# One block for adaLN conditioning and input projection, a third buffer of query weights, and 45 instead of 33 expert groups in the first tile's own routing

## The chip, the core and the metric

The kernel runs on one core of one Trainium2 chip. The metric is device time in microseconds for one execution. Five engines run their own instruction streams and meet at semaphores: TensorE (PE, with its weight loads as PEld), VectorE (DVE), ScalarE (ACT), GpSimd (POOL) and SyncE (SP), which only issues transfers. Sixteen DMA engines serve all transfers. All arithmetic is in 32-bit floats.

## What is computed

One layer of a decoder trunk, for 1024 prompt rows and for 32 sampled rows (8 sequences of 4), d_model = 1024. Cut to what matters here:

```
mod = c @ w_ada + b_ada            # 9 rows of c: one for the prompt, 8 for the sampled rows
shift1, scale1, gate1, shift2, scale2, gate2 = split(mod, 6)       # 1024 columns each
h = rms(x) * norm1_g * (1 + scale1) + shift1
q, k, v, f, glu = split(h @ w_in, [512, 1024, 1536, 1544])         # 2568 columns
A = forgetting attention over 8 heads of 64 (q and k normed, f gives the decay)
B = silu(layernorm(causal depthwise conv, 31 taps (a * sigmoid(b)))),   a, b = split(glu)
x1 = x + gate1 * (concat(A, B) @ w_o)
h2 = rms(x1) * norm2_g * (1 + scale2) + shift2
y = x1 + gate2 * peer(h2)

peer(h): per row and each of 8 retrieval heads:
    q = h @ w_query[head]                         # 256 columns
    the 16 best of 128 x 128 product keys -> 16 experts out of 16384, with softmax gates g
    sum over the 128 (head, expert) pairs of  g * gelu(h . expert_u[e]) * expert_v[e]
```

The experts are gathered from memory row by row: one row is expert_u and expert_v of one expert, 8 KB.

## The kernel before

Four functions run one after the other, each a block of its own with a stream for each engine; a block ends only when all its engines are done.

`condition` computes mod. SyncE loads w_ada in 12 chunks of 2 MB into three buffers `wa` (L112); TensorE makes 9 x 512 products (L157), VectorE copies them to `mod` (L187), TensorE transposes them into columns (`to_columns`, L147). Then VectorE adds the bias (`modT`, L190) and makes (1 + scale) * norm_g (`sgT`, L193 and L194). The two gates are spread over 128 rows for the prompt (L169) and over 32 rows for the sampled rows (L177) by TensorE, copied by VectorE (L202, L207) and stored (L119, L120). w_in, 10.3 MB, is issued as one transfer behind w_ada (L114).

`project` computes the norm, the modulation and h @ w_in, first for the 32 sampled rows, then for eight tiles of 128 prompt rows: `norm_x` on ScalarE and VectorE, `rows_up` (L555, transposes of x), the modulation into `hT` (VectorE at L459 and L462 for the sampled rows, ScalarE at L399 for prompt rows), then on TensorE the f columns (L572), q, k, v (L578), the two halves of the GLU columns (`gated`, L562) with `rows_up` of the next tile between them, and the transposes of q and k (L605, for the sampled rows L609), which ScalarE copies to `qTb` and `kTb` (L408, L412) for SyncE to store.

`sampled` does the attention of the sampled rows over their paged cache.

`tail` does all the rest. `iterate` writes one order for all engines: a tile has 55 steps (attention in 0 to 15, convolution, output product and norm in 16 to 34, routing from S_ROUTE = 35 on). Each tile's steps run beside the expert groups of the tile before: `PLAN` says how many of its 128 groups follow each step. A group is one gather of 128 expert rows (L1108, GpSimd, 1 MB, into one of the 8 slots of `ring`), a dot product on VectorE (L1515), gelu, gate and a diagonal on ScalarE (L1227, L1229, L1237) and four 128 x 64 matmuls on TensorE (L1670). A slot is free for the next gather when its matmuls are done. The first tile has no tile before it; `PLAN_0` puts groups of its own behind its last steps: as soon as head 0 has its experts and gates they begin, 33 in all, and the second tile's steps run beside the 95 that are left. In the routing TensorE needs the query weights of one head, 1 MB, every second step (L1651). `load_wq` on SyncE loads them (L994) into two buffers, each as soon as the head two before has been multiplied (`qd_done`). SyncE's order in a tile is: keys of heads 2 to 7, x, the eight weight loads, then `prefetch` of the next tile (q, mask, conv rows, the first two key loads), then the store of y.

The lines of this order that the change touches:

```python
PLAN_0 = [0] * (S_GATE + 1) + [2] * 12 + [3] * 3          # 33 groups

def load_wq(t, h):                                         # SyncE
    n = H * t + h
    if n >= 2:
        sp.wait_ge(qd_done, n - 1)
    sp.dma_start(wq[n % 2][:, :, :], ...).then_inc(wq_in[n % 2], 16)
```

Of the kernel before, what the change touches and what calls it, by code (L numbers as in the profile page):

```python
# [78 lines left out]
def condition(nc, I, S, K, w_in_load):  # L79
    with ExitStack() as ctx:  # L80
        sb = lambda n, s, d=F32: ctx.enter_context(nc.sbuf_tensor(n, s, d))
        sem = lambda n: ctx.enter_context(nc.semaphore(n))
        wa = [sb(f"wa{i}", [P, DC, 512]) for i in range(3)]
        cT = sb("cT", [P, DC, M])
        bT = sb("bT", [P, 48])
        ng = sb("ng", [P, 2, DC])
        gS, gate, gate_s = sb("gS", [P, 2, DC, TS]), sb("gate", [P, 2, D]), sb("gate_s", [TS, 2, D])
        mod = sb("mod", [M, 6 * D])
        wide = sb("wide", [P, 2 * SEQ - P], BF16)
        mod_bank = ctx.enter_context(nc.psum_tensor("mod_bank", [P, 512], F32))  # L90
        mod_ps = mod_bank[:, 0:48 * M].rearrange("p (n m) -> p n m", m=M)
        row_ps = [ctx.enter_context(nc.psum_tensor(f"row_ps{i}", [P, 512], F32)) for i in range(3)]
        gate_ps = [ctx.enter_context(nc.psum_tensor(f"gate_ps{i}", [P, 512], F32)) for i in range(4)]
        ada_in = [sem(f"c_w{i}") for i in range(3)]
        rows_copied, modT_done = sem("c_rows"), sem("c_modT")
        small_in, w_used, id_step = sem("c_small"), sem("c_used"), sem("c_id")
        own_v, gates, gates_out = sem("c_own"), sem("c_gates"), sem("c_gout")
        stored = sem("c_stored")
        wv = I["w_ada"].rearrange("(k p) n -> p k n", p=P)
        modT, sgT, ident = K["modT"], K["sgT"], K["ident"]  # L100
        NCH = 12
        block = ctx.enter_context(nc.Block())

        @block.sync
        def _(sp):
            sp.dma_start(cT[:, :, :], I["cT"]).then_inc(small_in, 16)
            sp.dma_start(bT[:, :], I["b_adaT"]).then_inc(small_in, 16)
            sp.dma_start(ng[:, :, :], I["norm_gT"]).then_inc(small_in, 16)
            for n in range(NCH):
                if n >= 3:  # L110
                    sp.wait_ge(w_used, n - 2)
                sp.dma_start(wa[n % 3][:, :, :], wv[:, :, n * 512:(n + 1) * 512]).then_inc(ada_in[n % 3], 16)  # L112

            sp.dma_start(K["w_in"][:, :, :], I["w_in"].rearrange("(k p) n -> p k n", p=P)).then_inc(w_in_load, 16)  # L114
            sp.wait_ge(id_step, 7)
            sp.dma_start(S["mask"], wide[:, :]).then_inc(stored, 16)
            sp.wait_ge(gates_out, 2)
            for g in range(2):
                sp.dma_start(S["gate"][g], gate[:, g, :]).then_inc(stored, 16)  # L119
                sp.dma_start(S["gate_s"][g], gate_s[:, g, :]).then_inc(stored, 16)  # L120
            sp.wait_ge(stored, 16 * 5)

        @block.gpsimd
        def _(pool):

            pool.memset(ident[:, :], 0.0).then_inc(id_step, 1)
            pool.memset(K["tri"][:, :], 1.0).then_inc(id_step, 1)
            pool.memset(K["ones"][:, :], 1.0).then_inc(id_step, 1)
            pool.memset(wide[:, :], 0.0).then_inc(id_step, 1)
            pool.wait_ge(id_step, 4)  # L130
            pool.affine_select(out=ident[:, :], in_=ident[:, :], compare_op=ALU.not_equal, fill=1.0, base=0,
# [1651 lines left out]
```

## Time and profile before

| | |
|---|---|
| median of 3 runs | 3870.56 us (3864.44 to 3872.29) |
| the profiled execution | 3873.22 us |
| its span, from first to last instruction | 3871.5 us |
| mean granted TensorE clock | 0.908 of full |
| TensorE busy | 3115.4 us |
| VectorE busy | 2471.7 us |
| ScalarE busy | 1550.2 us |
| GpSimd busy | 1283.3 us |
| DMA | 1291.75 MB, mean 334 GB/s over the span |

Busy time is the time in which an engine has an instruction under way. A window's row has, for each engine, its busy time and in brackets the number of its instructions, then the granted TensorE clock as a share of full speed, the mean busy share of the 16 DMA engines, and what they moved. The DMA share can come out at 1.01 or 1.02; that is full. In the page's rows of 40 slices a slice is 96.8 us, a digit the busy share in tenths (9 is 90% or more).

By the rows of the timeline, `condition` runs to about 122 us, `project` to about 530, `sampled` to 645, and `tail` from there; the first tile's routing ends at about 870, and a tile of the tail then takes some 370 us.

### The profile page before, as it was taken

Reading aid. Unit: us, or ns where it says so; the run is one execution under the profiler, and the core shown is the slowest. Engines: PE = TensorE matmul, PEld = TensorE weight load, DVE = VectorE, ACT = ScalarE, POOL = GpSimd, SP = SyncE. Lnnn points to the kernel's source line nnn. Section 1 sums busy time; section 2 is a strip of 40 time slices with the busy share of each in tenths; the row PEclk is TensorE's granted clock in tenths of the full one; section 3 lists DMA queues with packets and bytes.
Section 4 is the critical chain, followed back from the end, with each engine's and each line's share of the span. In section 5 each row is a group of like instructions: output and inputs, shape, how many; then the busy total and the mean of one; then the engine's idle time right before and its main releaser. Section 6 shows DMA issues by size and latency. Waiting matters only on the chain.

```text
span 3871.5 us, 44083 instructions
## 1 busy us (share of the span) xinstructions
PE 3115.4 (80%) x11624; PEld 1421.8 (37%) x11624; DVE 2471.7 (64%) x6411; ACT 1550.2 (40%) x4275; POOL 1283.3 (33%) x1139
## 2 busy tenths in 40 slices
PE   8699976578887887788688868887887788757877
PEld 2466742333342243224332433343334333411341
DVE  0222323488588677767776777587668766856785
ACT  0234411246425533543355345534552555233423
POOL 0000030034334343444344334443343334344433
PEclk9699987699998998899899989998998899979989
DMA  8211152389999999999999999999999999989998
GB/s 317 86 47 41 41 200 96 132 320 399 367 376 366 414 404 375 371 413 407 371 401 409 408 355 404 408 401 378 400 398 403 341 407 405 380 338 418 417 377 355
DMA packets 299720, 1291.75 MB, mean 334 GB/s; under 512 B 39270, under 2 KB 135414, under 8 KB 163124
## 3 DMA queue, kind: packets, MB, share of 16 engines
q0 software_dynamic: 156672, 1124.27, 72.3%
q1 hardware_dynamic: 142780, 164.51, 12.9%
q8 instruction: 93, 1.52, 0.2%
q14 instruction: 175, 1.43, 0.1%
HBM read 1271.34 MB, written 17.79 MB: 333 GB/s over the span
## 4 chain that ended last, share of the span: by engine, by line
DMA 34%; PE 21%; DVE 14%; issue 7%; ACT 5%; SPq 1%; POOL 1%; DVEq 0%; POOLq 0%; ACTq 0%
DMA ring<-experts_dram,idxc 22%; DMA wq<-w_query_dram 12%; PE YY L1670 12%; DVE ring L1515 5%; PE M L1651 4%; PE TT L1657 3%; DVE yac L1262 2%; SPq L1021 1%; ACT gw L1229 1%; ACT dg L1237 1%; ACT L1227 1%; DVE yac L1436 1%; PE SS L1546 1%; ACT ga L1227 1%; POOL ring L1108 1%
## 5 line engine op out<-in xcount | busy, mean ns | idle before, releaser
L1670 PE MATMUL YY<-ring,dg 128*64 128x512 f32 (+1 forms) x4224 | 1804.1, 655 | 486.0 <-ACT dg L1237 463.3
L1108 POOL DMA_INDIRECT ring<-experts_dram,idxc x1056 | 1233.4, 1168 | 1810.3 <-PE YY L1670 1608.0
L1515 DVE CUSTOM_DVE_ANT_0 ring<-ring,h2c 128x1024 f32<-128x1024 f32 x1056 | 1273.3, 1226 | 551.6 <-DMA ring<-experts_dram,idxc 542.2
L1670 PEld LDWEIGHTS YY<-ring,dg 128*64 128x64 f32 (+1 forms) x4224 | 502.1, 145 | 1576.3 <-ACT dg L1237 831.2
L1227 ACT ACTIVATE ga<-act 128x1 f32<-128x1 f32 x1056 | 210.6, 199 | 911.5 <-DVE act L1515 909.1
L1651 PE MATMUL M<-fT,wq 128*128 128x128 f32 (+1 forms) x2304 | 310.2, 299 | 96.3 <-DMA wq<-w_query_dram 96.3
L1237 ACT ACTIVATE dg<-fold,gw 128x64 f32<-128x64 f32 x1024 | 356.0, 348 | 51.0 <-ACT gw L1229 2.6
L1651 PEld LDWEIGHTS M<-fT,wq 128*128 128x128 f32 x2304 | 297.4, 213 | 155.7 <-DMA wq<-w_query_dram 122.4
L1229 ACT ACTIVATE gw<-ga,gc 128x1 f32<-128x1 f32 x1056 | 311.0, 295 | 35.1 <-ACT ga L1227 1.0
L1262 DVE SCALAR_TENSOR_TENSOR yac<-win,cw,yac 128x128 f32<-128x128 f32 x960 | 262.9, 346 | 2.5 <-issue 2.5
L1188 ACT ACTIVATE qh<-M 128x256 f32<-128x256 f32 x64 | 24.5, 383 | 462.4 <-PE M L1651 462.4
L578 PE MATMUL A<-w_in,hT 128*128 128x512 f32 (+1 forms) x432 | 193.5, 609 | 3.6 <-ACT kTb L408 3.6
L688 POOL DMA_INDIRECT pages<-cache_dram,k_idx x32 | 30.2, 944 | 408.2 <-POOLq L213 398.8
L1657 PE MATMUL TT<-w_o,fT 128*128 128x512 f32 (+1 forms) x288 | 138.5, 627 | 10.1 <-DVE fT L1437 6.8
L562 PEld LDWEIGHTS A<-hT,w_in 128*128 128x128 f32 x1152 | 141.1, 205 | 4.2 <-issue 4.2
L562 PE MATMUL A<-hT,w_in 128*128 128x128 f32 (+1 forms) x1152 | 141.9, 286 | 0.0
L1227 ACT ACT_TABLE_LOAD x96 | 123.2, 1283 | 13.0 <-DVE act L1515 11.4
L578 PEld LDWEIGHTS A<-w_in,hT 128*128 128x128 f32 (+1 forms) x432 | 79.2, 185 | 111.1 <-issue 106.9
L1546 PE MATMUL SS<-kh,t_qT 66*128 66x512 f32 (+1 forms) x192 | 88.0, 570 | 25.8 <-ACT h2c L1214 16.2
L1555 PEld LDWEIGHTS V<-V,t_PT 128*128 128x128 f32 x656 | 79.6, 194 | 52.2 <-issue 45.4
L157 PE MATMUL row_ps<-wa,cT 128*9 128x512 f32 x192 | 86.1, 603 | 10.3 <-DMA wa<-w_ada_dram 10.3
L1555 PE MATMUL V<-V,t_PT 128*128 128x64 f32 x656 | 88.8, 283 | 4.8 <-DMA V<-v_prompt_dram_out 4.4
(305 smaller groups left out, 2385.9 us busy)
## 6 DMA issues: line engine op xcount, KB each, us to landing
wq<-w_query_dram SPq DMA_DIRECT2D x72, 1024.0 KB, 27.0
wa<-w_ada_dram SPq DMA_DIRECT2D x12, 2048.0 KB, 7.9
ring<-experts_dram,idxc POOLq DMA_INDIRECT x1056, 13.7
w_in<-w_in_dram SPq DMA_DIRECT2D x1, 10272.0 KB, 34.1
kh<-kT_scratch SPq DMA_DIRECT2D x16, 264.0 KB
xb<-x_prompt_dram SPq DMA_DIRECT2D x8, 512.0 KB, 5.3
t_xb<-x_prompt_dram SPq DMA_DIRECT2D x8, 512.0 KB, 11.1
w_o<-w_o_dram SPq DMA_DIRECT2D x8, 512.0 KB, 5.5
```

The source lines that it names most:

```text
L562: mm = pe.matmul(A[half][:, (j % CC) * P:(j % CC) * P + r], w_in[:, k, ZG + j * P:ZG + (j + 1) * P], h[:, k, 0:r], start=(k == 0), stop=(k ...
L578: mm = pe.matmul(A[2 + j][0:r, :], h[:, k, 0:r], w_in[:, k, j * DA:(j + 1) * DA], start=(k == 0), stop=(k == DC - 1))
L1108: pool.indirect_dma_start(ring[:, k % RING, :], None, I["experts"], bass.IndirectOffsetOnAxis(idxc[:, k:k + 1], 0)).then_inc(g_in[k % RING ...
L1227: act.activation(ga[:, a:a + 1], act8[:, a:a + 1], ACT.Gelu).then_inc(gelu_done, 1)
L1229: act.activation(gw[:, a:a + 1], ga[:, a:a + 1], ACT.Copy, scale=gc[:, k:k + 1]).then_inc(gelu_done, 1)
L1237: act.activation(dg[:, k % DG, :], fold2[:, :], ACT.Copy, scale=gw[:, a:a + 1]).then_inc(diag_done, 1)
L1262: own.step(v.scalar_tensor_tensor(out_of(c), rows_of(c, k), cw[:, c, k:k + 1], out_of(c), ALU.mult, ALU.add))
L1515: v.tensor_tensor_reduce(out=u, in0=u, in1=h2, scale=1.0, scalar=0.0, op0=ALU.mult, op1=ALU.add, accum_out=act8[:, k % RING:k % RING + 1]) ...
L1555: mm = pe.matmul(V0[:, h * HD:(h + 1) * HD], PTs[:, b * P:(b + 1) * P], V[:, b, h * HD:(h + 1) * HD], start=(b == 0), stop=(b == nk // P - 1))
L1651: mm = pe.matmul(M0[:, g * P:g * P + r], wq[h % 2][:, k, g * NK:(g + 1) * NK], fT[:, k, 0:r], start=(k == 0), stop=(k == DC - 1))
L1657: mm = pe.matmul(TT[0:r, g * 512:(g + 1) * 512], fT[:, k, 0:r], w_o[:, k, g * 512:(g + 1) * 512], start=(k == 0), stop=(k == DC - 1), skip ...
L1670: mm = pe.matmul(YY[o, half * 512:(half + 1) * 512], dg[:, k % DG, 0:w], ring[:, k % RING, D + half * 512:D + (half + 1) * 512], start=(k ...
```

## The change

It has three parts.

1. `condition` and `project` become one block, `front`. `condition` no longer opens a block: it returns pieces of each engine's stream, which `front` places. The norm of x_sample runs at the start; `rows_up(0)`, its transposes, stands between the last row product and `to_columns(11)`. w_in is issued in nine pieces: the q, k, v and f columns of one 128-row slab behind each of the last eight w_ada chunks, and the GLU columns behind them. The gates are no longer spread on TensorE: 16 transposes give 9 rows of each gate, four copies put them where `qTb` and `kTb` will be, and the stores read one row 128 times (the prompt) or each of 8 rows 4 times (the sampled rows). TensorE waits for these copies ahead of the q, k, v product of the sampled rows; ScalarE waits for these stores ahead of its first write to `qTb`. `mod` holds two chunks instead of twelve and lies in `sqq`. VectorE waits for the projection's constants behind the norm of the first prompt tile, and makes the page indices behind the sampled rows.
2. `PLAN_0` has 3 groups behind each of its last 15 steps, 45 in all; the second tile's steps run beside 83.
3. The query weights have three buffers, head h in h % 3. The third shares its memory with the two key buffers `kh`: its load for head 2 waits until all scores of the tile are done, and the keys of the next tile wait for head 5's query.

The diff, cut to its core:

```diff
-def condition(nc, I, S, K, w_in_load):
+def condition(nc, ctx, I, S, K, R):
+    A, mod, gate = R["A"], R["mod"], R["gate"]
+    mod_ps = A[4][:, 0:48 * M].rearrange("p (n m) -> p n m", m=M)
+    row_ps, gate_ps = A[0:3], A[0:4]
...
             sp.dma_start(wa[n % 3][:, :, :], wv[:, :, n * 512:(n + 1) * 512]).then_inc(ada_in[n % 3], 16)
-            sp.dma_start(K["w_in"][:, :, :], I["w_in"].rearrange("(k p) n -> p k n", p=P)).then_inc(w_in_load, 16)
+            if n >= NCH - DC:
+                k = n - NCH + DC
+                sp.dma_start(K["w_in"][:, k, 0:ZG], wi[:, k, 0:ZG]).then_inc(R["w_qkv"], 16)
+        sp.dma_start(K["w_in"][:, :, ZG:DIN], wi[:, :, ZG:DIN]).then_inc(R["w_glu"], 16)
...
+        rows_up(0)
+        to_columns(NCH - 1)
+        pe.wait_ge(own_v, 1)
+        for g, first in ((0, 16), (1, 40)):
+            for half in range(2):
+                for c in range(4):
+                    mm = pe.transpose(gate_ps[2 * g + half][0:M, c * P:(c + 1) * P], modT[:, first + 4 * half + c, :],
+                                      ident[:, :])
+        mm.then_inc(modT_done, 1)
...
+    def vector_gates(v):
+        v.wait_ge(modT_done, NCH + 1)
+        for g in range(2):
+            for half in range(2):
+                v.tensor_copy(gate[g][0:M, half * 512:(half + 1) * 512], gate_ps[2 * g + half][0:M, :])\
+                    .then_inc(rows_copied, 1)
+    def store_gates(sp):
+        sp.wait_ge(rows_copied, NCH + 4)
+        for g in range(2):
+            sp.dma_start(S["gate"][g].unsqueeze(0), gate[g][0:1, :].unsqueeze(1).to_broadcast([1, P, D]))\
+                .then_inc(gates_out, 16)
+            sp.dma_start(S["gate_s"][g].rearrange("(n q) d -> n q d", q=QS),
+                         gate[g][1:M, :].unsqueeze(1).to_broadcast([NS, QS, D])).then_inc(gates_out, 16)
...
+    def gates_stored(eng):
+        eng.wait_ge(gates_out, 16 * 5)
+    def gates_read(eng):
+        eng.wait_ge(rows_copied, NCH + 4)
...
             sp.dma_start(xb[0:TS, :], I["x_sample"]).then_inc(x_in, 16)
+            c_sync(sp)
...
             load_x(1, 0)
+            store_gates(sp)
             store(0, 1, None, None)
...
                 if not isinstance(t, int) or t > 0:
                     act.wait_ge(stored_qk, 32 * t)
+                else:
+                    gates_stored(act)
...
                 if r == TS:
+                    c_rows(v)
...
                     v.sem_inc(hT_ready, 1)
+                    c_gates(v)
                 if more:
                     norm_x(t + 1)
...
                 if some(t):
                     pe.wait_ge(qkT_ready, t)
+                else:
+                    gates_read(pe)
...
+                if not some(t):
+                    pe.wait_ge(w_glu, 16)
                 gated(1, r, h)
...
-            pe.wait_ge(w_in_load, 16)
-            rows_up(0)
+            c_tensor(pe, rows_up)
+            pe.wait_ge(w_qkv, 16 * DC)
...
-PLAN_0 = [0] * (S_GATE + 1) + [2] * 12 + [3] * 3
+PLAN_0 = [0] * (S_GATE + 1) + [3] * 15
...
-        wq = [sb(f"wq{i}", [P, DC, 2 * NK]) for i in range(2)]
+        shared = sb("shared", [P, 2 * SEQ])
+        wq = [sb(f"wq{i}", [P, DC, 2 * NK]) for i in range(2)] + [shared[:, :].rearrange("p (k n) -> p k n", k=DC)]
-        kh = [sb(f"kh{i}", [AUG, SEQ]) for i in range(2)]
+        kh = [shared[0:AUG, i * SEQ:(i + 1) * SEQ] for i in range(2)]
...
             def load_wq(t, h):
-                n = H * t + h
-                if n >= 2:
-                    sp.wait_ge(qd_done, n - 1)
-                sp.dma_start(wq[n % 2][:, :, :], wqv[:, :, h * 2 * NK:(h + 1) * 2 * NK]).then_inc(wq_in[n % 2], 16)
+                b = h % 3
+                if h > 2:
+                    sp.wait_ge(qd_done, H * t + h - 2)
+                elif b == 2:
+                    sp.wait_ge(s_done, H * min(t + 1, NB))
+                elif t:
+                    sp.wait_ge(qd_done, H * t - 1 + b)
+                sp.dma_start(wq[b][:, :, :], wqv[:, :, h * 2 * NK:(h + 1) * 2 * NK]).then_inc(wq_in[b], 16)
...
                     sp.wait_ge(conv_done, t)
+                    sp.wait_ge(qd_done, H * t - 2)
...
-                    pe.wait_ge(wq_in[h % 2], 64 * t + 16 * (h // 2 + 1))
+                    b = h % 3
+                    pe.wait_ge(wq_in[b], 16 * ((2 if b == 2 else 3) * t + h // 3 + 1))
```

## Rows read from the trace of the kernel before

**Rows 1.** the page: DMA row in 40 slices; one line of its costliest groups
```profile
DMA  8211152389999999999999999999999999989998
...
L157 PE MATMUL row_ps<-wa,cT 128*9 128x512 f32 x192 | 86.1, 603 | 10.3 <-DMA wa<-w_ada_dram 10.3
```

**Rows 2.** windows by stage: busy time of each engine, granted clock, DMA share, GB/s
```profile
760.00:880.00 120.00, 85.81 (x313) 39.68 (x314) 102.40 (x333) 53.51 (x139) 40.91 (x38) 0.87 0.90 333
880.00:1185.00 305.00, 247.10 (x898) 105.24 (x896) 230.42 (x621) 139.84 (x381) 112.10 (x101) 0.93 0.96 372
1185.00:1555.00 370.00, 300.29 (x1028) 125.75 (x1028) 267.85 (x673) 163.76 (x475) 148.97 (x130) 0.91 1.00 398
```

**Rows 3.** timeline of TensorE: start, length, line, what, count [idle before <- releaser]
```profile
99.83 0.41 PE L147 MATMUL mod_bank<-ident,mod 9*128 9x9 f32 x4 [0.43 <-DVE mod L187]
...
136.50 1.03 PE L555 MATMUL A<-ident,xs 32*128 32x32 f32 x8 [22.78 <-DVE xs L445]
...
141.27 23.66 PE L578 MATMUL A<-w_in,hT 128*32 128x512 f32 x48
...
177.82 13.70 PE L562 MATMUL A<-hT,w_in 128*128 128x32 f32 x64
...
240.12 20.87 PE L578 MATMUL A<-w_in,hT 128*128 128x512 f32 x48 [0.45 <-ACT kTb L408]
```

**Rows 4.** timeline of VectorE, and of SyncE's queue in the last row
```profile
100.28 0.61 DVE L190 TENSOR_TENSOR modT<-mod_bank,bT 128x432 f32<-128x432 f32 x1 [0.51 <-PE mod_bank L147]
...
113.76 2.82 DVE L207 COPY gate_s<-gate_ps 32x512 f32<-32x512 f32 x4 [5.50 <-PE gate_ps L177]
...
140.09 0.19 DVE L462 TENSOR_TENSOR hT<-hT,modT 128x32 f32<-128x32 f32 x1
...
77.58 0.58 SPq L114 DMA_DIRECT2D w_in<-w_in_dram  x1
```

**Rows 5.** DMA issues: queue, count, KB each, median us from issue to landing
```profile
wq<-w_query_dram SPq DMA_DIRECT2D x72, 1024.0 KB, 27.0
wa<-w_ada_dram SPq DMA_DIRECT2D x12, 2048.0 KB, 7.9
...
w_in<-w_in_dram SPq DMA_DIRECT2D x1, 10272.0 KB, 34.1
...
gate_scratch<-gate SPq DMA_DIRECT2D x2, 512.0 KB, 3.5
```

**Rows 6.** windows in the front
```profile
40.00:60.00 20.00, 20.00 (x57) 4.71 (x56) 2.04 (x3) 0.00 (x0) 0.00 (x0) 1.00 0.82 279
95.00:100.00 5.00, 4.57 (x17) 1.21 (x15) 0.68 (x1) 0.00 (x0) 0.00 (x0) 1.00 1.01 427
170.00:175.00 5.00, 5.00 (x25) 5.00 (x25) 3.54 (x10) 2.45 (x3) 0.00 (x0) 0.50 0.00 0
```

**Rows 7.** timeline of VectorE: one head in the first tile's routing
```profile
802.73 0.49 DVE L1285 MAX8 best<-sc 128x8 f32<-128x128 f32 x2
...
805.94 1.22 DVE L1515 CUSTOM_DVE_ANT_0 ring<-ring,h2c 128x1024 f32<-128x1024 f32 x1
...
818.49 0.48 DVE L1285 MAX8 best<-sc 128x8 f32<-128x128 f32 x2
```

**Rows 8.** TensorE's waits (us, times, longest); windows at two of the stalls
```profile
PE M L1651 <- DMA wq<-w_query_dram: 96.3, 18, 10.0
...
1480.00:1490.00 10.00, 10.00 (x43) 7.26 (x43) 3.94 (x7) 2.16 (x9) 1.12 (x2) 0.74 0.72 266
3690.00:3700.00 10.00, 10.00 (x30) 4.84 (x32) 1.80 (x12) 3.80 (x15) 1.87 (x2) 0.65 0.79 256
```

**Rows 9.** timeline of GpSimd at a tile's boundary; windows at two boundaries
```profile
1567.16 0.94 POOL L1108 DMA_INDIRECT ring<-experts_dram,idxc  x1 [17.23 <-PE YY L1670]
...
1160.00:1175.00 15.00, 6.19 (x13) 1.95 (x12) 13.52 (x37) 5.57 (x13) 4.36 (x4) 0.77 0.50 186
3770.00:3780.00 10.00, 7.45 (x20) 3.08 (x22) 7.95 (x19) 8.06 (x22) 4.45 (x4) 0.73 0.53 194
```

More of the change, by code:

```diff
@@ L213, in project, with front @@
+def front(nc, I, O, S, K):
     with ExitStack() as ctx:
@@ L255, in project @@
         ident = K["ident"]
+        w_qkv, w_glu = sem("p_wqkv"), sem("p_wglu")
+        flat = lambda a: a[:, :, :].rearrange("p h t -> p (h t)")
+        c_sync, c_gpsimd, c_tensor, c_rows, c_gates, store_gates, gates_stored, modulation_ready, gates_read = condition(
+            nc, ctx, I, S, K, {"A": A, "mod": sqq[:, :].rearrange("p (g n) -> p g n", g=2),
+                               "gate": [flat(qTb), flat(kTb)], "w_qkv": w_qkv, "w_glu": w_glu})
         block = ctx.enter_context(nc.Block())
@@ L314, in _ @@
             sp.dma_start(O["conv_prompt"], ub[P - (W - 1):P, :]).then_inc(once_out, 16)
+            gates_stored(sp)
             sp.wait_ge(once_out, 16 * 3)
@@ L321, in _ @@
         def _(pool):
+            c_gpsimd(pool)
             pool.memset(zero[:, :, :], 0.0).then_inc(cst, 1)
@@ L397, in body @@
                     act.wait_ge(xT_done, t + 2)
+                    if not some(t):
+                        modulation_ready(act)
                     for c in range(DC):
@@ L414, in body @@
                 a.then_inc(qkT_ready, 1)
+            norm_x(0)
             act.wait_ge(own_p, 5)
-            norm_x(0)
             body(0, 0)
@@ L465, in body @@
                     v.sem_inc(hT_ready, 1)
+                    c_gates(v)
                 if more:
                     norm_x(t + 1)
+                if not some(t):
+                    v.wait_ge(own_p, 5)
+                    v.wait_ge(small_in, 80)
                 own.start(OVN * (t + 2) + OV * t if more else OVN * (t + 1) + OV * t)
@@ L527, in body @@
                 assert own.n == OV, own.n
-            v.wait_ge(own_p, 5)
-            v.wait_ge(small_in, 80)
+            norm_x(0)
+            body(0)
             v.wait_ge(paged, 1)
@@ L535, in _ @@
                 .then_inc(lane_ready, 1)
-            norm_x(0)
-            body(0)
             body(1)
@@ L584, in body @@
                     u_rows(TS)
+                if not some(t):
+                    pe.wait_ge(w_glu, 16)
                 gated(1, r, h)
@@ L965, in tail @@
         k_in = [sem(f"k{i}") for i in range(2)]
-        wq_in = [sem(f"wq{i}") for i in range(2)]
+        wq_in = [sem(f"wq{i}") for i in range(3)]
         smp_in, gate_in = sem("smp"), sem("gate")
@@ L1732, in build @@
                     K[name] = early.enter_context(nc.sbuf_tensor(name, shape, F32))
-                condition(nc, I, S, K, w_in_load)
-                project(nc, I, O, S, K, w_in_load)
+                front(nc, I, O, S, K)
             sampled(nc, I, O, S, K)
```

195 lines of the change are left out of this document (75 added, 120 removed).

## The prediction

> **What bounds the kernel now.** I read the page's DMA row first [rows 1], then the time by stage [rows 2], and only then single instructions. The DMA row says that there are two kernels in this one. From slice 9 on it stands at 9 in almost every slice; before that it mostly doesn't. The stage table gives the same in numbers: from 1185 to 1555 us, one whole tile of prompt rows in the tail, the DMA share is 1.00 at 398 GB/s, and so it goes for seven tiles. A tile takes 128 gathers of 128 rows of 8 KB (1.05 MB each) and eight 1 MB weight loads, and its length is what the DMA engines need for these bytes. A faster step in there is worth only the DMA idle time that it removes. From 760 to 880 us, the routing of the first tile, the share is 0.90. Between 110 and 530 us (digits 1 and 2 of the DMA row) the front runs on TensorE, with the DMA engines hardly used.
>
> So I price each part in one of two ways: in the front by the chain of instructions that leads to the projection, in the tail by DMA idle time, with a share of 1.00 as full.
>
> **Part 1, one block.** Now: the columns of the last row product are transposed at 99.83 to 100.24, then TensorE does gates only, and it is idle for 22.8 us before 136.50; the first q, k, v product begins at 141.27 [rows 3]. In between lie the gates, their stores, the end of the block, a new load of x_sample and its norm. The changed chain, step by step. Loading x_sample first puts one issue ahead of the weights: +0.4. Eight transposes of x_sample (1.03 at 136.50) go between the last product and the last columns, where TensorE waits 0.43 for a copy: +0.6 at most, I take 0.3. So modT starts at 100.28 [rows 4] + 0.7 = 101.0 and takes 0.61; four operations on a sixth of its elements have to follow, an estimate of 0.25 each: 102.6. The sixteen operations that modulate the sampled rows run from the end of their transposes at 137.5 to 140.28, 2.7 us: 105.3. The new wait of TensorE for the gate copies stands ahead of q, k, v; behind it on TensorE is everything. VectorE makes these four copies behind the modulation, 2.8 us by the four copies of the same size at 113.76: 108.1. The 16 gate transposes, by 8 in 1.03 us some 2 us, are done by then. The product starts at about 108.2 instead of 141.27: **33.1 us saved**.
>
> This needs the weights by 108. Today w_in is issued at 77.58 [rows 4], behind all of w_ada, and lands 34.1 us later, at 112 [rows 5]; with that it would be the end of the chain. The change issues its q, k, v, f columns in eight pieces of 0.79 MB, one behind each of the last eight w_ada chunks. TensorE uses one chunk in 7.3 us (86.1 us for twelve products [rows 1], and their transposes); the DMA share at that pace is 0.82 with 279 GB/s, and larger packets reach 427 GB/s a little later [rows 6]. A chunk then costs 0.82 x 7.3 = 6.0 us, a piece 0.79/0.42 = 1.9 us, 7.9 together. That is 0.6 us over the period, 4.8 us in eight periods; a chunk lands 7.9 us after its issue [rows 5] and is needed 14.6 us after it, a slack of 6.7. So it just fits, the last chunk with some 2 us to spare and the last piece at about 92; the GLU columns (4.2 MB, 10 us) follow by 103 and are needed at about 130. I price this at 0, and at 5 us if the slack is gone.
> The Trainium skill (DMA: Bandwidth & Descriptors, Specifications) speaks against this part: it puts what one core gets from HBM at about 358 GB/s. By it, 2.89 MB would take 8.1 us per period, 6.2 us over eight, and nearly the whole slack would go. The trace shows 427 GB/s on this core, so the row decides, and the sum is left as it is.
>
> The clock: q, k, v of the sampled rows took 23.66 us, of the second prompt tile 20.87 [rows 3], and I put the difference down to the idle 22.8 us ahead of it. The change leaves TensorE idle for two times of about 2 us there. I take half of the 2.8 us: **1.4**, between 0 and 2.8.
> The projection's constants, the mask and the index arithmetic move behind other work on SP and VectorE, and GpSimd's memsets of the projection run 100 us earlier, where it is idle; the first x_prompt rows land at about 106 and are transposed only after the first half of the GLU products, at about 145. Cover: 40 us of TensorE work. Stored gates: below, a rival. Part 1: **34.5 us** (28 to 37).
>
> **Part 2, 45 groups instead of 33 in the first routing.** One head there takes VectorE 802.73 to 818.49, 15.8 us, with four groups of 1.22 [rows 7]: VectorE is the bound. Twelve more groups add 12 x 1.22 = 14.7 us. In the DMA's time they cost 12 x 1.05 MB / 0.40 = 31 us; the stretch has 0.10 x 120 = 12 us idle [rows 2] plus the 14.7 new ones, so it grows by some 19 us, and the next tile, with 83 groups left, is 31 us shorter if it stays bound by DMA (share 0.96 now). Net 12, all the idle time of the stretch; as a head then needs 7.3 MB in 18.2 us (403 GB/s) it will not fill without seams: **10 us** (-15 to 12).
>
> **Part 3, the third weight buffer.** TensorE waits 96.3 us in all for query weights, 18 times, up to 10 us [rows 8]. It is tempting to book these 96 us. But while it waits, the gathers go on until the eight slots of the ring are full, and only then do the DMA engines idle: the stall that ends at 1480 leaves a share of 0.72 for 10 us, 2.8 us of idle time. There are seven such stretches, the last at 3690; they sum to 19 us the first and the last in [rows 8], and one at 1100 adds 2. With three buffers head 2 is loaded during attention, and each later load is issued three head times ahead of its use and not two; a head takes some 14 us there, so 41 us stand against the median of 27.0 from issue to landing [rows 5], where 28 stand against it now. So the stalls should be gone. The new wait on SP (all scores of the tile done) is met some twenty steps before the routing, and has only the other weight loads behind it. The next tile's keys wait for head 5's query; today the last weight load, which stands ahead of them, waits for the same count. Bound: 0 to 60 us. I take the idle time at the stalls: **20 us**.
> What is late next: the tile's boundary. From the last group of a tile to the first of the next GpSimd waits up to 17.2 us for a slot, and the share falls, to 0.50 for 15 us at 1160. Nine such places hold 42 us, the first and the last in [rows 9]. That chain (softmax, gates, the copy of h2) is not touched.
>
> **Sum.** 34.5 + 10 + 20 = 64.5 us. The profiled execution took 3873.2 us (span 3871.5), 2.7 over the median of 3870.6. 3873.2 - 64.5 - 2.7 = **3806 us**.
>
> **Rivals.**
> (a) The forecast, 45%: 3806, by its own bounds 3795 to 3815.
> (b) The buffer brings nothing, 23%: the DMA engines, no longer stopped in the routing, come to the boundary further ahead, and what was idle at the stalls is idle there. For it: boundaries idle twice as much already as the stalls. Against it: those boundaries have some slack (one idles 1.3 us only). 3826.
> (c) The buffer also clears boundaries, 13%: a routing without stalls finishes its indices earlier, the next tile's gathers start earlier. Of the 42 us, 10 belong to the loads of the sampled rows; were all the rest gained, 3774.
> (d) Part 2 does not pay, 10%: the first routing grows by 14.7 and more, and the next tile doesn't shrink, since its steps wait for each other (its share is 0.96 already [rows 2]). Then -34.5 + 15 - 20: 3831.
> (e) The sampled rows' GLU runs at the full clock, 5%. Its second half takes 13.70 us [rows 3], at a granted 0.50 [rows 6]; if the earlier pause were the cause, the two halves could give back some 10 us: 3796. Against it: the granted clock is 0.50 in 170 to 175 with TensorE busy 5.00 of 5.00 us [rows 6], 30 us after the pause, and after q, k, v had run almost at the pace of a later tile; what changed in between are the matmuls, narrow ones of 32 columns. The Trainium skill (TensorE: Matmul & The Clock Gate, Part 1) says that activity releases the throttle; read as busy time, that would give (e), and this row speaks against such a reading.
> (f) Slower than before, 4%: the gate stores. One partition is now the source of 128 rows of 4 KB, twice, and of 0.26 MB more. ScalarE waits for them before it may write q and k of the sampled rows, and TensorE's next tile waits for that. Today's stores read 128 partitions and land in 3.5 us [rows 5]. They are issued at about 108.5; the q, k copy comes behind the second GLU half, which ends at 191.5, 50 us after q, k, v began [rows 3], so at about 158: 50 us are free. It costs nothing down to 1.3 MB / 50 us = 26 GB/s, about what one of 16 engines moves at 420 GB/s, and decides the sign once the stores take 115 us, at 11 GB/s; at 10 GB/s it gives 3887.
>
> **Range and chances.** (a), (b), (d), (e) and most of (c) are within 3770 to 3836: somewhat over 8 in 10, and the two bounds of parts 1 and 2 are inside with them. A measurement of this kernel tells 0.2% (8 us) from no change. Only (f) is no gain: faster 0.95, same 0.01, slower 0.04.
>
> **What would show it.** Part 1: the first q, k, v product at 107 to 110, no gap in the row products from 26 to 99; a gap there, and the weights came late. If the first transposes of q and k are followed by a wait of ScalarE, it is (f). Part 2: the first routing ends about 19 us longer than it was, some 15 us earlier in all, and the next tile is about 31 us shorter. Part 3: the 96.3 us of TensorE waiting for query weights go to near 0 and seven tiles are 2 to 4 us shorter each; if instead GpSimd's waits at the boundaries grow, it is (b). The prediction is wrong at its root if tiles shrink by 10 us or more each: then not bytes but the chain was the bound.

## The result and the profile after

| | before | after |
|---|---|---|
| median, runs taken side by side | 3867.5 us | 3835.85 us (3832.87 to 3840.74) |
| ratio to before | 1 | 0.992, interval 0.990 to 0.994 |
| profiled execution, and its span | 3873.2 us, 3871.5 us | 3832.9 us, 3831.0 us |
| mean granted TensorE clock | 0.908 | 0.915 |

The change saves 31.6 us where I forecast 64.5. The sign was right, the size was not: 3836 is the upper edge of my range. The two profiled executions lie some 40 us apart, since the one before was the slowest of its four and the one after the fastest; differences of a few us between single traces are therefore read beside the timed runs. I read the profile after in the order of the prediction: the front, the first tiles, the weight loads.

**The front.** Timeline of TensorE in the kernel after (start, length, line, what, count, and in brackets the idle time before it and who ended it); it answers [rows 3]:

```profile
100.23 0.66 PE L565 MATMUL A<-ident,xs 32*128 32x32 f32 x8
100.80 0.41 PE L138 MATMUL A<-ident,sqq 9*128 9x9 f32 x4
101.91 1.92 PE L159 MATMUL A<-ident,modT 128*9 128x128 f32 x16 [0.70 <-DVE modT L172]
...
108.26 22.11 PE L590 MATMUL A<-w_in,hT 128*32 128x512 f32 x48 [1.82 <-DVE kTb L183]
...
141.60 13.70 PE L572 MATMUL A<-hT,w_in 128*128 128x32 f32 x64
```

VectorE in the same stretch, answering [rows 4], with the last of the sixteen operations that modulate and the gate copies behind it:

```profile
101.25 0.61 DVE L172 TENSOR_TENSOR modT<-A,bT 128x432 f32<-128x432 f32 x1 [0.51 <-PE A L138]
...
105.41 0.19 DVE L470 TENSOR_TENSOR hT<-hT,modT 128x32 f32<-128x32 f32 x1
105.74 1.28 DVE L183 COPY qTb<-A 9x512 f32<-9x512 f32 x2
106.94 1.27 DVE L183 COPY kTb<-A 9x512 f32<-9x512 f32 x2
```

The q, k, v product begins at 108.26, where the forecast had 108.2. The saving stays whole up to the tail. The tail's first load, in SyncE's timeline of the kernel before:

```profile
645.80 0.88 SPq L1008 DMA_DIRECT2D t_qT<-qT_scratch  x1
```

and of the kernel after, with the stores of y of the first and the last prompt tile behind it:

```profile
612.21 0.89 SPq L1028 DMA_DIRECT2D t_qT<-qT_scratch  x1
...
1139.92 0.37 SPq L1075 DMA_DIRECT2D y_prompt_dram_out<-yb  x1
...
3743.07 0.36 SPq L1075 DMA_DIRECT2D y_prompt_dram_out<-yb  x1
```

So 33.6 us are saved when the tail begins. The same two stores stand in SyncE's timeline of before:

```profile
1182.14 0.37 SPq L1055 DMA_DIRECT2D y_prompt_dram_out<-yb  x1
...
3784.29 0.36 SPq L1055 DMA_DIRECT2D y_prompt_dram_out<-yb  x1
```

The seven tiles between them took 2602.2 us before and take 2603.2 after. Whatever the third buffer did, it did not shorten them.

Between the tail's first load and the first of these stores this pair of traces shows 536.3 us before and 527.7 after, 8.6 less, in the stretch that part 2 changes. The timed runs below do not bear that out. In the traces of the experiments the same stretch takes 532.0 and 534.5 us without part 2 (e3 and e1), 531.2 and 533.5 with it (e2 and e4): this pair lies at the two ends of what single executions show.

**The first two tiles.** Windows of the kernel after, columns as in [rows 2]: the first routing, the second tile, one steady tile, and the end of the second tile's routing:

```profile
724.00:838.00 114.00, 84.00 (x324) 38.40 (x324) 103.25 (x325) 51.77 (x143) 45.19 (x43) 0.87 1.01 396
838.00:1143.00 305.00, 245.46 (x886) 104.30 (x886) 230.82 (x634) 141.86 (x377) 103.59 (x97) 0.91 0.92 354
1143.00:1507.00 364.00, 294.96 (x1028) 122.18 (x1028) 267.21 (x671) 163.16 (x474) 148.37 (x130) 0.93 1.01 402
1115.00:1130.00 15.00, 7.67 (x17) 2.23 (x18) 13.70 (x39) 3.57 (x13) 2.68 (x3) 0.73 0.21 72
```

Set these against [rows 2] and [rows 9]. The share in the first routing rose from 0.90 to 1.01: its idle time is filled. The second tile's window has to start at the same event as in the kernel before, just behind VectorE's last search of experts in the first routing:

```profile
861.00:1185.00 324.00, 260.95 (x934) 110.24 (x934) 245.12 (x657) 151.26 (x413) 119.40 (x107) 0.92 0.94 366
```

So the share of the second tile fell from 0.94 to 0.92, and at that tile's end it is 0.21 for 15 us, where it was 0.50 before. Part of the idle time has changed its place. GpSimd's timeline says what it waits for there, the expert indices of the next tile:

```profile
1126.12 0.23 POOL L1121 COPY idxc<-idxn 128x64 int32<-128x64 int32 x1 [12.64 <-DVE idxn L1365]
```

In the kernel before, the longest such wait was 8.7 us.

The last search itself, in VectorE's timeline of the kernel before and of the kernel after:

```profile
857.65 0.43 DVE L1313 MAX8 top<-cand 128x8 f32<-128x256 f32 x1
```

```profile
834.47 0.43 DVE L1333 MAX8 top<-cand 128x8 f32<-128x256 f32 x1
```

From the tail's first load to it the first routing took 211.9 us and takes 222.3, 10 us longer where I had forecast 19. From there to the first store of y it was 324.5 us and is 305.5, 19 us shorter where I had forecast 31.

**The weight loads.** Rows of the list of waits of the kernel after (total us, times, longest), against [rows 8]:

```profile
POOL ring L1128 <- PE YY L1691: 1619.7, 577, 23.6
...
POOL idxc L1121 <- DVE idxn L1365: 39.8, 7, 12.6
...
PE M L1672 <- DMA wq<-w_query_dram: 56.9, 11, 8.9
```

the first two of them in the kernel before:

```profile
POOL ring L1108 <- PE YY L1670: 1608.0, 560, 22.3
...
POOL idxc L1101 <- DVE idxn L1345: 41.0, 7, 8.7
```

and the DMA issues of the kernel after (count, KB, median us from issue to landing), against [rows 5]:

```profile
wq<-w_query_dram SPq DMA_DIRECT2D x54, 1024.0 KB, 32.1
wa<-w_ada_dram SPq DMA_DIRECT2D x12, 2048.0 KB, 9.9
shared<-w_query_dram SPq DMA_DIRECT2D x18, 1024.0 KB, 37.2
...
w_in<-w_in_dram SPq DMA_DIRECT2D x8, 772.0 KB, 11.4
```

TensorE's wait fell by 39 us only, not to zero, and a load now takes 32 to 37 us where it took 27. In the chain of work that ended last, the load issued at 1418.86, a last head's, stands with 46 us:

```profile
1418.86 46.23 DMA wq<-w_query_dram
```

TensorE waits for it until it lands at 1465.1. The last such wait of the kernel after ends at 3702.8, and the DMA engines idle behind it more than behind the wait of before in [rows 8] (0.79 for 10 us):

```profile
3705.00:3720.00 15.00, 15.00 (x50) 8.59 (x50) 7.37 (x24) 4.44 (x17) 2.97 (x4) 0.65 0.48 181
```

So I added up the DMA engines' idle time by place, from windows of 5 us: from 150 to 25 us before each of the last seven stores of y, where TensorE waits for query weights, and from 25 us before to 60 us after each of the eight stores, the boundaries of the tiles.

| idle DMA time, us | before | e3, part 3 alone | after | g1, before with packed weights |
|---|---|---|---|---|
| at the waits for weights | 19.9 | 23.1 | 23.6 | 1.5 |
| at the boundaries | 46.2 | 46.7 | 49.1 | 55.1 |

(e3 and g1 are experiments below; e1, e2 and e4, which have two buffers and weights in 1 KB pieces like the kernel before, have 19.6 to 25.0 in the first row.) The third buffer took none of the idle time away that it was meant to take. It left fewer waits, later in the routing, with as much DMA idle time behind them.

### The profile page after: what moved, and what is told of

The parts are those of the page before. It is cut to its first block, busy times and chain, and to the rows that moved or that the text cites. A ratio compares the mean times of both kernels' runs of the same rounds, so it can differ in the third digit from the quotient of the medians.

```text
span 3831.0 us, 44007 instructions
## 1 busy us (share of the span) xinstructions
PE 3097.5 (81%) x11576; PEld 1397.2 (36%) x11576; DVE 2464.9 (64%) x6391; ACT 1551.8 (41%) x4275; POOL 1260.0 (33%) x1139
## 4 chain that ended last, share of the span: by engine, by line
DMA 31%; PE 20%; DVE 18%; issue 8%; ACT 6%; SPq 1%; POOL 1%; DVEq 0%; another core or an unknown queue 0%; POOLq 0%; ACTq 0%
DMA ring<-experts_dram,idxc 23%; PE YY L1691 11%; DMA wq<-w_query_dram 7%; DVE ring L1535 6%; PE M L1672 3%; PE TT L1678 3%; DVE yac L1282 1%; SPq L1041 1%; ACT gw L1249 1%; ACT dg L1257 1%; DVE eq L1338 1%; DVE eq L1341 1%; DVE sel L1343 1%; PE SS L1566 1%; ACT L1247 1%
## 5 line engine op out<-in xcount | busy, mean ns | idle before, releaser
L1128 POOL DMA_INDIRECT ring<-experts_dram,idxc x1056 | 1211.6, 1147 | 1830.0 <-PE YY L1691 1619.7
L1672 PE MATMUL M<-fT,wq 128*128 128x128 f32 (+1 forms) x1728 | 225.1, 293 | 56.9 <-DMA wq<-w_query_dram 56.9
L1672 PEld LDWEIGHTS M<-fT,wq 128*128 128x128 f32 x1728 | 215.5, 207 | 99.3 <-DMA wq<-w_query_dram 67.7
L1566 PE MATMUL SS<-shared,t_qT 66*128 66x512 f32 (+1 forms) x192 | 89.3, 577 | 25.3 <-ACT h2c L1234 15.8
L147 PE MATMUL A<-wa,cT 128*9 128x512 f32 x192 | 86.5, 605 | 10.8 <-DMA wa<-w_ada_dram 10.8
```

The source lines that it names most:

```text
L1128: pool.indirect_dma_start(ring[:, k % RING, :], None, I["experts"], bass.IndirectOffsetOnAxis(idxc[:, k:k + 1], 0)).then_inc(g_in[k % RING ...
L1672: mm = pe.matmul(M0[:, g * P:g * P + r], wq[b][:, k, g * NK:(g + 1) * NK], fT[:, k, 0:r], start=(k == 0), stop=(k == DC - 1))
```

## The experiments

Times are medians of timed runs of a kernel, beside runs of the kernel before on the same chip.

**One part at a time.** e1 is part 1 alone, e4 parts 1 and 2. e2 changes only this line of the kernel before:

```diff
-PLAN_0 = [0] * (S_GATE + 1) + [2] * 12 + [3] * 3
+PLAN_0 = [0] * (S_GATE + 1) + [3] * 15
```

e3 takes only the `wq`, `kh`, `load_wq` and `prefetch` lines of the change, with TensorE's wait for `wq_in`.

> Only part 1: one block, with 33 groups and two weight buffers. If the front is worth what its chain of instructions says, the time is 33 to 36 us below the kernel before (3832 to 3835) and the first expert group starts 33 to 36 us earlier; the tiles after it keep their lengths. If the tail takes a part of the front's gain back (since its transfers meet in another order), the gain is under 28 us and the tiles are longer.

> Only part 2: 45 groups in the first routing. As predicted (idle DMA time of the first routing is filled, none lost elsewhere): 10 us below the kernel before. By the rival that the second tile does not shrink fully, because its own boundary idles more: 0 to 5 us below; then the DMA idle time of the first routing is near 3 us and that of the second tile about 9 us more than before.

> Only part 3: the third buffer of query weights. By the prediction 20 us below the kernel before. By the rival that now has the changed kernel's trace for it (the idle time at the stalls turns up at the tiles' boundaries, and the last two heads still wait because the loads queue behind each other): within 5 us of the kernel before, with TensorE's waits for weights at 50 to 65 us instead of 96, and the time from issue to landing above 30 us instead of 27.

> The changed kernel without the third buffer (parts 1 and 2). If the third buffer is worth nothing, this runs as the changed kernel does, 3832 to 3840. If the buffer is worth 20 us, it is at 3856. If the buffer costs something (more weight loads in flight beside the gathers), this one is faster than the changed kernel, at 3825 to 3830.

| | median us | ratio to before (interval) |
|---|---|---|
| e1, part 1 | 3831.8 | 0.989 (0.988 to 0.991) |
| e2, part 2 | 3869.5 | 0.999 (0.998 to 1.001) |
| e3, part 3 | 3872.2 | 1.000 (0.999 to 1.002) |
| e4, parts 1 and 2 | 3835.4 | 0.990 (0.989 to 0.992) |

The whole gain is part 1. Parts 2 and 3 are each worth nothing, within 0.2%.

The traces show how part 2 cancels. With 12 groups more, the first routing is 10.9 us longer in e2 than before and 15.8 longer in e4 than in e1; the second tile is 16.0 and 16.6 us shorter. That is 1.4 us for a group taken out of the second tile, not 2.6.

In e3 TensorE's wait for weights nevertheless fell from 96.3 to 58.3 us (list of waits of e3):

```profile
PE M L1658 <- DMA wq<-w_query_dram: 58.3, 10, 10.3
```

so 38 us less waiting on the engine bought no time at all. The table above says why: the DMA engines idle at these waits as before.

**Packed weights.** Two theories were left for part 3. Either the tail's bound is elsewhere, or the loads stay slow whatever is buffered, since each moves pieces of 1 KB and shares the DMA engines with gathers of 8 KB pieces. f1 is the kernel after with w_query laid out head by head in memory, so that a load has 8 KB pieces; f2 is the same with two buffers. The array is put in this order before the timed kernel starts.

```diff
-            wqv = I["w_query"].rearrange("(k p) n -> p k n", p=P)
+            wqv = I["w_query"]
...
-                sp.dma_start(wq[b][:, :, :], wqv[:, :, h * 2 * NK:(h + 1) * 2 * NK]).then_inc(wq_in[b], 16)
+                sp.dma_start(wq[b][:, :, :], wqv[:, h, :, :]).then_inc(wq_in[b], 16)
...
-        "w_o": g["w_o"][0], "w_query": g["peer_w_query"][0],
+        "w_o": g["w_o"][0], "w_query": g["peer_w_query"][0].reshape(DC, P, H, 2 * NK).transpose(1, 2, 0, 3),
```

> The changed kernel with w_query laid out by head, so that a weight load reads 8 KB in one piece per partition instead of eight pieces of 1 KB; bytes, buffers and waits are the same. Theory 1 (a weight load competes with the gathers packet by packet, so its time goes with its number of packets, and loads queue behind each other): from issue to landing falls from 32 us to 10 us or less, and TensorE's waits for weights from 57 us to under 5. Theory 2 (the time is set by its bytes only): it stays at 30 us. For the time of the kernel: if stalls on weights cost what they idle, 15 to 20 us less than the changed kernel; if that idle time moves to the boundaries, within 5 us of it, unless large packets also save time on the DMA engines themselves.

> The same layout with two weight buffers (parts 1 and 2 and the layout). By theory 1 its loads also land in 10 us and TensorE does not wait for them either, so it runs within 3 us of f1_packed: the third buffer is then of no use at all. If a third buffer matters for another reason than the stalls, f1_packed is faster by 5 us or more.

f1 took 3809.9 us (ratio 0.985, 0.983 to 0.987), f2 3796.3 (0.982, 0.980 to 0.983). That is 26 and 39 us less than the same kernels with 1 KB pieces. Neither has a wait of TensorE for weights in its list. g1 is the kernel before with this one edit:

> The kernel before, but the query weights lie in memory head by head, so that a 1 MB load moves pieces of 8 KB instead of 1 KB; nothing else is changed. Theory: small pieces are what makes a load slow beside the gathers and what costs the DMA engines time of their own. Then the gain doesn't depend on parts 1 and 2: with both it was 3835.4 - 3796.3 = 39 us, so here 3869 - 39 = 3830, no wait of TensorE for query weights over 1 us, and a steady tile of the tail some 6 us shorter. Rival: the gain of the packed weights came out of the stretches that parts 1 and 2 changed (the first tile's routing): then it is under 25 us here.

It took 3826.6 us, ratio 0.990 (0.988 to 0.992): 41 us, about as much as part 1. The page of the kernel before has, for its DMA packets and its queues (packets, MB, share of 16 engines' span; q0 holds the gathers, q1 what SyncE issues):

```profile
DMA packets 299720, 1291.75 MB, mean 334 GB/s; under 512 B 39270, under 2 KB 135414, under 8 KB 163124
...
q0 software_dynamic: 156672, 1124.27, 72.3%
q1 hardware_dynamic: 142780, 164.51, 12.9%
```

and of g1, with its weight loads from the DMA issues:

```profile
DMA packets 235208, 1291.75 MB, mean 338 GB/s; under 512 B 39270, under 2 KB 61686, under 8 KB 89396
...
q0 software_dynamic: 156672, 1124.27, 73.1%
q1 hardware_dynamic: 78268, 164.51, 11.9%
...
wq<-w_query_dram SPq DMA_DIRECT2D x72, 1024.0 KB, 9.1
```

The bytes are the same; 64512 packets are gone. Queue q1's time fell from 12.9% of 3871.5 to 11.9% of 3821.9, 499 to 455 us: some 45 us less DMA time (the shares are rounded to 0.1%, 4 us each). The span fell by 50, but 7 of these lie ahead of the tail (its first load is issued at 638.93 and not 645.80), where this edit does nothing; the tail is 43 us shorter, 38 of them in the seven tiles between the stores of y. A load lands in 9.1 us, not 27. In the two traces a packet of 1 KB took 49 ns on average, so eight of them 392 ns, and one of 8 KB on the same queue 320 ns. So most of this gain is DMA time and not waiting, and a MB in 1 KB pieces costs about 0.6 us more of it than in 8 KB pieces (45 us / 72 loads). From the windows of 5 us, one less their DMA share, the idle time of the seven steady tiles sums to 63.8 us before, 66.3 after, 55.1 in g1: with no wait for weights left, idle time fell by 9 us, not by 20. The table by place shows the rest: 18 us went at the waits for weights, 9 came back at the boundaries.

**How many groups belong in the first routing.** With packed weights, part 1 and two buffers: 33 groups (g2), 15 (g3), 45 (f2, above). g3 against g2:

```diff
-PLAN_0 = [0] * (S_GATE + 1) + [2] * 12 + [3] * 3
+PLAN_0 = [0] * (S_GATE + 1) + [1] * 15
```

> Part 1 and packed query weights, 33 groups in the first routing, two buffers. Theory: 45 groups instead of 33 only move work between two stretches, also when the weights come early: the same as with 45, 3796 within 5 us. Rival (part 2 pays once the second tile's steps no longer wait for weights): 10 us slower than with 45, 3806.

> As g2_front_packed, but 15 groups in the first routing instead of 33. The first routing is 18 x 1.22 = 22 us shorter, since VectorE sets its pace. Theory (groups moved between the two stretches are worth nothing either way, because the second tile has idle DMA time that takes them up): within 5 us of g2. Rival (the second tile is bound by the DMA engines): 18 x 1.05 MB / 0.40 = 47 us longer there, so 25 us slower in all.

g2 took 3796.2 us (ratio 0.981, 0.979 to 0.983), g3 3798.8 (0.982, 0.980 to 0.984), f2 3796.3: no difference for 15, 33 or 45. VectorE's last search of experts in the first routing and SyncE's store of the first tile's y show how they cancel. g3, 15 groups:

```profile
804.84 0.43 DVE L1327 MAX8 top<-cand 128x8 f32<-128x256 f32 x1
...
1144.34 0.36 SPq L1069 DMA_DIRECT2D y_prompt_dram_out<-yb  x1
```

f2, 45 groups:

```profile
837.48 0.43 DVE L1327 MAX8 top<-cand 128x8 f32<-128x256 f32 x1
...
1144.16 0.36 SPq L1069 DMA_DIRECT2D y_prompt_dram_out<-yb  x1
```

Thirty groups more make the first routing 32.6 us longer and the stretch from its end to that store 32.8 us shorter: 1.1 us for a group on either side. Not the 2.6 us of DMA time that I had given back for it.

**The tile boundary.** f3 is the kernel after with two of the finished tile's groups put ahead of the next tile's step 0, to shorten the chain that makes its last slots free; f4 adds packed weights.

```diff
+EARLY = 2
...
         begin(t - 1)
         for s in range(STEPS):
+            if s == 0:
+                for k in range(EARLY):
+                    group(t - 1, done + k)
             step(s, t, nk)
...
-            for k in range(upto[s], upto[s + 1]):
+            for k in range(max(upto[s], EARLY), upto[s + 1]):
                 group(t - 1, done + k)
```

> The changed kernel with the first two groups of the finished tile ahead of step 0 of the next tile's steps instead of behind it, on all engines: the boundary gets shorter by one attention step, some 5 to 8 us per tile. If DMA idle time at the boundaries is what takes the gains back, they idle less (42 us now) and the kernel is 15 to 40 us faster than the changed one. If the tail is bound by bytes alone and the idle time turns up in another place, within 5 us.

> Both edits together: no stalls on weights and a shorter boundary. If the idle time only moves between the two places, this is the kernel in which it can move to neither, and the gain is larger than the sum of the two alone: 25 to 60 us below the changed kernel. If bytes bound it, within 5 us of the better of the two.

f3 took 3839.3 us and f4 3812.9, against 3835.9 and 3809.9 without the edit: nothing gained, 3 us lost if anything. The order of these groups isn't what the boundary waits for; what is stays open.

**What the third buffer costs once loads are fast.** f1 is 14 us slower than f2. g5 is g2 with the third buffer:

> As g2_front_packed, but with the third buffer of query weights in the memory of the key buffers. Theory: the third buffer costs time once loads are fast, since the keys of the next tile now wait for head 5's query and the load of head 2 for the scores, and nothing is gained for it: 7 to 14 us slower than g2_front_packed (with 45 groups it was 3809.9 against 3796.3). Rival (that difference came from the 45 groups together with the buffer, or from the chip): within 4 us of g2_front_packed.

3808.4 us, 12 more than g2. h1 only puts the key buffers where they lie with three weight buffers; h2 has three buffers, whose loads go out as late as with two (against g5):

```diff
-                if h > 2:
-                    sp.wait_ge(qd_done, H * t + h - 2)
-                elif b == 2:
+                if b == 2:
                     sp.wait_ge(s_done, H * min(t + 1, NB))
+                if h >= 2:
+                    sp.wait_ge(qd_done, H * t + h - 1)
```

> As g2_front_packed (3796.2: part 1, packed weights, 33 groups, two weight buffers), but the two key buffers are slices of the array `shared`, which stands ahead of the weight buffers, as with three buffers. Theory (the earlier issue of the loads costs the time): as g2_front_packed, 3796 within 4 us. Rival (where the buffers lie costs it): 3808, as g5_front_third_packed.

> As g5_front_third_packed (3808.4: three weight buffers), but the load of head h is issued when head h-2 has been multiplied, as with two buffers, and not a head earlier; head 2 waits for the scores too, which is met long before. Theory (the earlier issue costs the time): 3796 within 4 us. Rival (the memory shared by keys and weights, or the rotation of three): 3808.

h1 took 3795.2, h2 3795.0. So memory and rotation cost nothing; the earlier issue costs the 12 us. (These kernels ran on different chips, but the kernel before beside them took 3867.7, 3866.6 and 3867.6 us.) i1 lets only head 2's load go early, i2 only the others:

> As g5_front_third_packed (3808.4), but the loads of heads 3 to 7 are issued as late as with two buffers; only head 2's load goes out early, when the scores are done. If head 2's load in the attention costs the time: 3808 within 4 us. If the others do: 3796.

> As g5_front_third_packed (3808.4), but head 2's load waits for head 0's query, as with two buffers; heads 3 to 7 are issued when head h-3 has been multiplied. If the others, a head time earlier each, cost the time: 3808 within 4 us. If head 2's load does: 3796. Both at about 3802: each load that comes earlier costs its share.

i1 took 3800.3 us (3795.5 to 3803.4), i2 3805.3 (3804.5 to 3808.1). The greater part, some 10 us, is with heads 3 to 7; head 2's share, 0 to 5 us, can't be told from nothing. The lists of waits go with that. h2, i1 and i2, in this order:

```profile
POOL ring L1128 <- PE YY L1691: 1525.6, 567, 23.2
```

```profile
POOL ring L1128 <- PE YY L1691: 1537.3, 583, 23.6
```

```profile
POOL ring L1129 <- PE YY L1692: 1558.5, 581, 23.1
```

GpSimd waits 33 us longer for slots with the early loads of heads 3 to 7, and 13 us less for its indices (49.2 after 62.6); the seven tiles take 2576.1 us in i2 and 2566.2 in h2. Why they do is not shown: loads land as fast (9 to 10 us), and q1 has the same 12.8% in g2, g5, h2 and i2.

## Why the prediction was right in one part and wrong in two

**Part 1: right, step by step.** Forecast and trace: transposes of x_sample between the last products, modT at 101.0 and 101.25, modulation done at 105.3 and 105.60, gate copies 2.8 and 2.5 us, product at 108.2 and 108.26, its own length 1.4 us shorter and 1.55 (granted clock 0.93 from 108 to 130, where it was 0.87 from 141 to 165). The price of 0 for the weights held: VectorE's copies end TensorE's last wait, not w_in. The slack was thinner than I had it, as a chunk of w_ada lands in 9.9 us and not 7.9, but TensorE's idle time for w_ada is 10.8 us after 10.3 [rows 1]. Forecast 34.5, trace 33.6 at the tail's start. The timed pairs give 30 (g1 to g2) to 38 (before to e1); in g1's trace the tail begins 7 us earlier than before, which may be most of that gap.

**Rival (f) was right in kind, and its cover held, with less room than I gave it.** The gate stores are the ones that read one partition 128 times, or 8 partitions 4 times each. From SyncE's timeline after, with a window of the same stretch:

```profile
108.24 0.59 SPq L189 DMA_DIRECT2D gate_scratch<-qTb  x1
...
109.66 15.16 SPq L189 DMA_DIRECT2D gate_scratch<-kTb  x1
124.87 9.72 SPq L191 DMA_DIRECT2D gate_s_scratch<-kTb  x1
134.63 13.43 SPq L277 DMA_DIRECT2D v_sample_dram_out<-vb  x1
```

```profile
108.00:148.00 40.00, 39.74 (x151) 23.14 (x151) 7.68 (x24) 14.43 (x29) 1.96 (x6) 0.80 0.91 31
```

For 40 us all DMA engines are busy (0.91) and move 31 GB/s. A packet of 4 KB takes 1.98 us there on average, and 0.19 us when the next rows of x_prompt are loaded at 158. The last of these packets ends at 148.5, and the queue is held up as long; ScalarE first writes `qTb` at 156.32, behind TensorE's transposes and not behind the stores. So some 8 us were left of a cover that I had put at 50. (f) had the price at which it starts to cost as 26 GB/s; 31 is close to it. Rival (e) did not come: the second GLU half still takes 13.70 us.

**Part 2: the wrong step is "31 us shorter if it stays bound by DMA".** The first half came about: the idle time of the first routing is filled. But I priced the groups taken out of the second tile by their DMA time, 2.6 us each, because its share was 0.96. It is not bound so: the tile became 16 to 19 us shorter by 12 groups, and g3 and f2 show 1.1 us for a group on either side. This price is near the 1.22 us of VectorE [rows 7] that I used for the first routing, so the second tile's steps and groups are bound by an engine or by their own chain (which of the two was not tried), and the DMA engines idle at its end until the next indices are there. The sign of a move between two such stretches is set by the difference of the two prices, and that is 0 within what the timed runs can tell. Rival (d) named the mechanism, but priced it as a loss of 15: it let the second tile shrink by nothing. The term was 10 and measured 0.

**Part 3: two steps were wrong.** The first is "41 us stand against the median of 27.0", and with it "so the stalls should be gone". I took the time from issue to landing as fixed. It grows with the number of loads under way, and a third buffer puts more of them there. Taken one by one from the traces: before, 25 loads were issued with no other under way and landed in 23.4 us (median), 47 with one and took 28.2; after, it is 22.8 with none, 38.1 with one, 47.4 with two (11 loads). That is why the last heads still wait, 56.9 us in all, and why the DMA engines idle at these waits no less than with two buffers (23.6 us, where before, e1, e2 and e4 have 19.6 to 25.0). The runs with 8 KB pieces (9 us, whatever the buffers) show that it was never the memory's own latency. The Trainium skill (DMA: Bandwidth & Descriptors, Queues, rings and completion order) says that each DMA engine takes turns between its queues packet by packet; that agrees with loads in pieces an eighth the size of the gathers' being served slowly beside them. An estimate from the traces fits too: if an engine took one piece of a load (49 ns) and one of a gather (325 ns) in turn, its 64 pieces of a load would take 64 x 374 ns = 23.9 us. No run here looks into the order of single packets.

The second is booking the stalls' idle time as gain. In the kernel after it can't be tested, since that idle time never went. g1 tests it: there no weight is waited for, the idle time at these places fell from 19.9 to 1.5 us, and that at the boundaries rose from 46.2 to 55.1. In all g1 saved 9 us of idle time, so 20 was twice too much even for a perfect cure. Rival (b) thus had part 3's result right, and by luck: its mechanism, idle time that moves to the boundaries, took back half in g1, but is not seen in e3 (46.2 to 46.7) nor in the kernel after (49.1, with 49.5 in e4, which has no third buffer). Rival (c), boundaries that clear, did not come in any of them.

With parts 2 and 3 both at nothing my own sum gives 3873.2 - 34.5 - 2.7 = 3836.0, the measured time; that it fits to 0.2 us is luck, since the sum starts from 3870.6 and the runs taken side by side have 3867.5 for the kernel before. I had not formed that case: (b) kept part 2's 10 us and (d) kept part 3's 20. The two depend on one premise, that the tail's time is the DMA engines' busy time plus an idle time that can be removed piece by piece, so they had to be allowed to fail together. The low bounds of my three parts, 28 - 15 + 0 = 13 us, give 3858; the range ended at 3836 as if they could not meet.

**What I overlooked** was in the page all along: "its length is what the DMA engines need for these bytes" is true only for packets of one size. Of the 299720 packets of the kernel before 45 in 100 are smaller than 2 KB, and the 73728 of the weight loads carry 75 MB. The Trainium skill (DMA: Bandwidth & Descriptors, Specifications) has line rate from 512 B on. By that row, 1 KB pieces would cost the same as 8 KB pieces and g1 would gain nothing in DMA time; the runs show 45 us of DMA time and 41 us of the kernel's, so here the measurement decides.

A version that beats both kernels came out of this: part 1, packed weights and two buffers (g2), 3796.2 us, a ratio of 0.981 to the kernel before. It differs from the kernel after by undoing parts 2 and 3 and by the order of w_query in memory.

## What to carry to other kernels

Where DMA engines are full nearly all the time, price an edit by the DMA time it removes (bytes, and packets of each size), and an idle stretch that is filled as zero until you can say which later stretch becomes shorter. A median from issue to landing is no latency while other loads share the queue: more buffers put more loads in flight, and each takes longer, so look where the idle time is after the change and not only at how long an engine waits. And two terms of a sum that rest on one premise need a rival in which both fall.

## What the runs showed of the hardware that I had not expected

- A 1 MB load beside the gathers lands in 9.1 us in pieces of 8 KB and in 27.0 us in pieces of 1 KB, and costs about 0.6 us less of all 16 DMA engines.
- Issuing packed weight loads one head time earlier, with landing time and DMA time unchanged, made the kernel 10 to 13 us slower (i2 and g5 against h2).
- Stores that read one partition 128 times, or 8 partitions 4 times each, keep all DMA engines at 0.91 for 40 us at 31 GB/s, 1.98 us for a packet of 4 KB. They hold SyncE's queue too: the issues behind them took 15.2, 9.7 and 13.4 us, where the stores of q, k and u of the same rows took 0.6 each.
- The more 1 MB loads in 1 KB pieces are under way beside the gathers, the longer each takes: 23 us with none other, 38 with one, 47 with two in the kernel after.
